# A decoder step on one core: the third normalization moved into the feed-forward before it, and the scan's opening rewritten

## What is computed

```
x = x + mixer(rmsnorm(x, norm_mix[layer]))
x = x + square(relu(rmsnorm(x, norm_mlp[layer]) @ w_up[layer])) @ w_down[layer]
```

```
z, xbc, dt = split(h @ w_in)            # h = rmsnorm(x), 1024 -> 2048 + 4096 + 32
xbc  = silu(causal_conv(xbc))           # four taps per channel, with history for the samples
dt   = softplus(dt + dt_bias)           # step sizes, one per head (32) and token
acs  = cumsum(dt * a) per chunk of 128  # exp(acs), exp(acs_end - acs), exp(acs_end): decays
# then, chunk after chunk, the scan over the states of 8 groups of 4 heads, gating by silu(z), norm
```

## Time and profile before

| | us |
|---|---|
| median of three runs | 3750.37 |
| profiled execution | 3743.06 |
| its span | 3741.4 |

### The profile page before, as it was taken

The page is one execution under the profiler, slowest core; times in us unless marked ns, Lnnn a source line. Parts: engine busy times, 40 slices in busy tenths (PEclk is TensorE's granted clock), DMA queues, the critical chain, the costliest instruction groups (busy, mean ns, idle before and its releaser), DMA issues. The chain is left out here.

```text
span 3741.4 us, 57050 instructions
## 1 busy us (share of the span) xinstructions
PE 3350.8 (90%) x20488; PEld 3116.8 (83%) x20488; DVE 1534.1 (41%) x2721; ACT 1138.1 (30%) x2092; POOL 1188.1 (32%) x849
## 2 busy tenths in 40 slices
PE   5779978975699999999679999999859999999998
PEld 5559963664599999999578888998849999999998
DVE  4489972333222121212336666666641221212122
ACT  3412212342332122222224555545531231312132
POOL 2015831212132222222215655545444322222222
PEclk9979988987799999999879999999969999999999
DMA  3017654003211111111232122222224111111111
GB/s 121 20 38 126 195 167 138 1 18 113 76 48 46 45 50 46 45 45 50 48 87 75 59 89 86 75 91 86 86 74 140 45 48 46 45 45 50 45 45 68
DMA packets 345874, 263.82 MB, mean 71 GB/s; under 512 B 55926, under 2 KB 311942, under 8 KB 344038
## 3 DMA queue, kind: packets, MB, share of 16 engines
q1 hardware_dynamic: 328102, 228.50, 20.7%
q10 hardware_dynamic: 10496, 15.81, 1.9%
q0 software_dynamic: 7168, 18.08, 1.4%
HBM read 219.43 MB, written 44.76 MB: 71 GB/s over the span
## 5 line engine op out<-in xcount | busy, mean ns | idle before, releaser
L232 POOL TENSOR_TENSOR w_low_sb<-w_loaded_sb,w_high_sb 128x1024 fp32r<-128x1024 f32 (+1 forms) x278 | 570.6, 2060 | 1761.2 <-ACT w_high_sb L224 1743.3
L250 PE MATMUL psum<-act_high_sb,w_high_sb 128*128 128x344 f32 (+1 forms) x2544 | 817.0, 321 | 24.0 <-PEq L188 17.1
L250 PE MATMUL psum<-act_low_sb,w_high_sb 128*128 128x344 f32 (+1 forms) x2544 | 815.3, 320 | 0.0
L250 PE MATMUL psum<-act_high_sb,w_low_sb 128*128 128x344 f32 (+1 forms) x2544 | 815.0, 320 | 0.0
L250 PE MATMUL psum<-second_high_sb,w_high_sb 128*128 128x344 f32 x1704 | 546.0, 320 | 0.0
L250 PE MATMUL psum<-second_low_sb,w_high_sb 128*128 128x344 f32 x1704 | 544.8, 320 | 0.0
L250 PE MATMUL psum<-second_high_sb,w_low_sb 128*128 128x344 f32 x1704 | 544.8, 320 | 0.0
L250 PEld LDWEIGHTS psum<-act_high_sb,w_high_sb 128*128 128x128 f32 (+1 forms) x2544 | 478.8, 188 | 26.0 <-issue 25.7
L250 PEld LDWEIGHTS psum<-act_high_sb,w_low_sb 128*128 128x128 f32 (+1 forms) x2544 | 479.2, 188 | 0.4
L250 PEld LDWEIGHTS psum<-act_low_sb,w_high_sb 128*128 128x128 f32 (+1 forms) x2544 | 478.7, 188 | 0.4
L224 ACT CAST w_high_sb<-w_loaded_sb 128x1024 fp32r<-128x1024 f32 (+1 forms) x230 | 239.9, 1043 | 671.3 <-PE psum L250 601.4
(11 more groups left out here) (419 smaller groups left out, 4655.3 us busy)
## 6 DMA issues: line engine op xcount, KB each, us to landing
w_loaded_sb<-in_w_up SPq DMA_DIRECT2D x64, 512.0 KB, 4.1
w_loaded_sb<-in_w_down SPq DMA_DIRECT2D x64, 512.0 KB, 3.7
w_loaded_sb<-in_w_in_odd SPq DMA_DIRECT2D x48, 512.0 KB, 4.0
key_pages_sb<-in_cache_k SPq DMA_DIRECT2D x64, 256.0 KB, 2.8
ecay_sum_spread_sb<-decay_sum_scratch SPq DMA_DIRECT2D x8, 2048.0 KB, 9.7
w_loaded_sb<-in_w_in_even SPq DMA_DIRECT2D x28, 512.0 KB, 4.1
x_scratch<-x_sb SPq DMA_DIRECT2D x2, 4128.0 KB, 13.2
x_sb<-x_scratch SPq DMA_DIRECT2D x2, 4128.0 KB, 14.9
```

Source lines behind the costliest of these rows:

```text
L232: ins = self.nc.gpsimd.tensor_tensor(self.wl[:, par, k, 0:width], self.wf[:, par, k, 0:width], self.wh[:, par, k, 0:width].bitcast(F32), A ...
L250: ins = nc.tensor.matmul(out, w[:, par, k, 0:width], a[:, k, cols], start=n == 0, stop=n == 3 * KT - 1)
```

## The change

1. **Normalization folded.** `layer_tail` of layer 0 gets `after=mixed`, a `Fold` for the third normalization, which writes its tiles into the pair of tiles `second`. The eight down units of the last group carry its work. `first_unit` gets a width, and the unit of the step sizes (32 columns) is it, inside `layer_tail`, with `act_rstd` behind.
2. **Small loads and the store moved.** `load_small` (ten of the small loads) stands on SP between the projection's loads and those of the feed-forward; `keep_x` stores x tile by tile behind the last down units, and loads the first two weights of the next block. The other three small loads (history, `expand`, the shifted samples) come in the next block, once unit 0 there is done.
3. **Opening.** Unit 0 of group 0 multiplies the unnormalized pair, and DVE multiplies by the root as it empties the banks. Beside it the normalized tiles are made, in place, and unit 1 takes them tile by tile (`second_unit`). ACT empties unit 1 after the softplus.
4. **Small work between the units.** History is turned before and after tile 6 (of 18 column tiles, i = 3 e + t), the step sizes after tile 9, sums and sample values after tile 11, the decays on ACT before the copy of tile 12. DVE does its shares between the convolutions.
5. `time_steps` and its block are gone; several buffers share other places.

```diff
...
+class Steps:
...
+    def load_small(self, sp):
...
+            for n, name in enumerate(("dt_bias", "a_log", "d_skip")):
+                sp.dma_start(self.sm[:, n:n + 1], B.i[name].rearrange("o h -> h o")).then_inc(self.s_small, 16)
+            for j in range(CW):
+                sp.dma_start(B.cw[:, :, j], B.i["conv_w"][0, j].rearrange("(c p) -> p c", p=P)).then_inc(self.s_small, 16)
...
+    def keep_x(self, sp):
+        B, u = self.B, self.u
+        for k in range(KT):
+            if k == KT - 2:
+                B.load_weights(sp, u, self.par, self.w_in[:, :, COL_DT:COL_DT + NH], NH)
+            if k == KT - 1:
+                B.load_weights(sp, u + 1, 1 - self.par, self.w_in[:, :, COL_X:COL_X + P])
+            sp.wait_ge(B.s_tile_free, (u - KT + k) * 3 + 9)
+            sp.dma_start(B.x_scratch[:, k, :], B.x[:, k, :]).then_inc(self.s_keep, 16)
...
+    def second_unit(self, pe):
...
+        for k in range(KT):
+            pe.wait_ge(self.s_high, k + 1)
+            self.await_low(pe, k)
             for t in range(NT):
...
+    def act_softplus(self, act):
...
+        nc.scalar.activation(self.raw[:], self.raw[:], ACT.Identity, bias=sm[:, 0:1]).then_inc(self.s_bias, 1)
...
+    def dve_normed(self, dve):
...
+        dve.wait_ge(self.s_keep, 16 * KT)
+        fold.await_rstd(dve)
+        for k in range(KT):
+            nc.vector.scalar_tensor_tensor(out=B.x[:, k, :], in0=B.x[:, k, :], scalar=B.gains[:, fold.gain, k:k + 1],
+                                           in1=fold.rstd[:], op0=ALU.mult, op1=ALU.mult).then_inc(self.s_normed, 1)
+            if k == 1:
+                for t in range(NT):
+                    B.await_tile(dve, self.u, t)
+                    nc.vector.tensor_tensor(self.raw[:, tcols(t)], B.tile(self.par, t, NH), fold.rstd[0:NH, tcols(t)],
+                                            ALU.mult).then_inc(self.s_raw, 1)
...
+            if k >= 1 and k - 1 not in self.POOL_K:
+                low(k - 1)
...
@@ mamba_groups, SP @@
+            def opening():
+                load_unit(0, 1)
+                load_unit(0, 2)
+                steps.load_history(sp)
+                for e in range(3, 6):
+                    load_unit(0, e)
+                steps.store_sums(sp)
+                load_unit(1, 0)
+                steps.await_stored(sp)
...
@@ mamba_groups, POOL @@
+            def opening():
+                steps.pool_low(pool, 0)
+                B.split_low(pool, unit(0, 1), par(1), pieces=2)
+                for k in steps.POOL_K[1:]:
+                    steps.pool_low(pool, k)
...
@@ mamba_groups, PE @@
+            def opening():
+                B.multiply(pe, unit(0, 0), par(0), steps.fold.high, steps.fold.low)
+                steps.second_unit(pe)
+                steps.turn_history(pe, 0)
+                for i in range(6, 18):
+                    tile(0, i // 3, i % 3)
+                    if i == 6:
+                        steps.turn_history(pe, 1)
+                    if i == 9:
+                        steps.turn_steps(pe)
+                    if i == 11:
+                        steps.sum_steps(pe)
+                pe.wait_ge(steps.s_sumc, 5)
+                pe.wait_ge(steps.s_chc, 2)
+                turn_conv_rows(0)
...
@@ mamba_groups, ACT @@
+            def opening():
+                high = lambda e: B.split_high(act, unit(0, e), par(e))
+                for k in range(KT):
+                    steps.act_high(act, k)
+                    if k == 2:
+                        high(1)
+                high(2)
+                steps.act_softplus(act)
+                act.wait_ge(B.s_tile_free, unit(0, 0) * 3 + 9)
+                for i in range(3, 18):
...
+                    if i == 12:
+                        steps.act_decays(act)
+                    evacuate(0, i // 3, i % 3, bank=3 * par(1) if i < 6 else 0)
...
@@ mamba_groups, DVE @@
+            def opening():
+                steps.dve_normed(dve)
+                for t in range(NT):
+                    B.await_tile(dve, unit(0, 0), t)
+                    nc.vector.tensor_tensor(pre[:, 0, PAD + t * TT:PAD + (t + 1) * TT], B.tile(par(0), t),
+                                            steps.fold.rstd[:, tcols(t)], ALU.mult).then_inc(B.s_tile_free, 1)
...
+                steps.dve_steps(dve)
+                steps.dve_history(dve)
+                convolve(0, 0)
+                steps.dve_rows(dve)
+                convolve(0, 1)
+                steps.dve_sums(dve)
+                convolve(0, 2)
+                steps.dve_decay(dve)
+                convolve(0, 3)
...
```

More of the change, by code:

```diff
@@ L700, in act @@
                 high(last, 0, 9 + k)
+            elif behind is not None:
+                behind()
             if self.after:
@@ L2193, in _ @@
             projected.act(act)
-            feed.act(act, kept=(lambda k: rows.kept(act, k)) if rows else None)
+            feed.act(act, kept=(lambda k: rows.kept(act, k)) if rows else None, behind=(lambda: steps.high_first(act)) if steps else None)
+            if steps:
+                steps.high_second(act)
+                after.act_rstd(act, steps.u)
             if rows:
@@ L2455, in part @@
                 if nx is not None:
-                    for e in range(0 if g is None else 1, 6):
+                    for e in range(1, 6):
                         load_unit(nx, e)
@@ L2501, in finish @@
                                gst[:]).then_inc(s_gout, 16)
+            def opening():
[3 more added lines that the diff above has]
+                    steps.pool_low(pool, k)
+                for e in range(2, 6):
+                    B.split_low(pool, unit(0, e), par(e), pieces=2)
+                B.split_low(pool, unit(1, 0), par(0), pieces=2)
+                pool.wait_ge(steps.s_dend, 1)
+                pool.wait_ge(steps.s_exp, 4)
             def part(g, nx, more):
-                splits = [] if nx is None else [0, 1, 2, 3] if g is None else [1, 2, 3]
+                splits = [] if nx is None else [1, 2, 3]
                 if g is not None:
```

446 lines of the change are left out of this document (264 added, 182 removed).

## The result

The changed kernel took 3683.93, 3686.55, 3690.90 and 3702.31 us, a median of **3688.7**; the kernel before took 3748.48 to 3753.21 in four runs, median 3750.2. The ratio is 0.984, with a 95% interval of 0.982 to 0.987. The forecast was 3691.8, and faster by 58.6; it is faster by 61.5.

What follows compares the result with a forecast made beforehand. Bound by TensorE, busy 90% of the span; gains lie where it stands still between first feed-forward and group scan. Stretch 162.5 to 103.9 us saves 58.6 from the 3750.37 median: 3691.8 us, range 3682 to 3705.

Steps and rivals of the forecast that it cites:

- Step sizes' unit with sums, 14.7: Unit of 32 columns right after the last down matmul, sums of squares included: 14.7 us without a gap.
- First unit 11.3, to 27.0: Group scan's first unit, on unnormalized tiles after the block change: 11.3 us without waiting for the normalization, ending at 27.0.
- Chain 22.9 + 4.0 = 26.9: Normalized tiles made beside the first unit: 22.9 us as before, 4.0 for added weight split and multiplies; last low tile 42.6.
- The copy behind the softplus frees the third unit, 47.7: ACT empties the second unit only after its softplus; the first copy frees a bank for the third unit at 47.7 us.
- Four units, small matmuls, clock: 45.2 + 8.5 + 2.5 = 56.2: Rest of the opening on PE: four units 45.2 us, small matmuls between them 8.5, clock loss after idling 2.5; end 103.9.
- Nothing from the convolutions, the decays, the small loads or the store: Other work in the opening, the early small loads and the tile-by-tile store of x stay covered: cost 0.
- C: Rival: early small loads make the feed-forward's first weights 14 us late, once; 3706 us; chance 0.03.
- 58.6 for the stretch: Last down matmul to conv-row transposes falls from 162.5 to 103.9 us, 58.6 less, all leaving the total.
- Rival A: Normalization's chain and ACT's queue take longer, as POOL's work can hold DVE: 7.2 us plus clock's 2.5; 3701; chance 0.15.
- B: Rival: small work between PE, DVE and ACT stalls the opening's units, 12.6 us more; 3704; chance 0.10.
- D: Rival: last eight down units lose weight lookahead, about 10 us each, 82 in all; slower, 3774; chance 0.02.
- E: Rival: copies not held by the softplus, small work at its best; opening ends at 97, no clock loss; 3685; chance 0.10.

Runs made afterwards that it cites:

- The run without a fall of the clock: Changed kernel with copies before softplus, all low halves on VectorE, second unit's weight split behind two normalized tiles: stretch 95.9 us, median 3691.5 us.
- the run with both edits: Changed kernel with ScalarE's copies of the second unit ahead of the softplus and all eight low halves on VectorE: stretch 100.9 us, median 3681.9 us.
- the run with the copy first: Changed kernel with ScalarE emptying the second unit's three tiles before the softplus: stretch 101.3 us, median 3696.5 us.

## Why the prediction was right

Its steps, from T = 0:

- **Step sizes' unit with sums, 14.7.** Measured 14.66, no wait. **Block change 1.0:** 0.64 on PE.
- **First unit 11.3, to 27.0.** It ended at 26.9.
- **Chain 22.9 + 4.0 = 26.9.** Measured 25.2. The added part was 2.3, not 4.0. The three multiplies took 2.0 of it (1833.87 to 1835.83), which leaves some 0.3 for GpSimd's weight split, given 2.4; no run takes that split out. The last low half came at 40.45 (42.6), ScalarE's last high one at 38.2 (40.4). The unit ended 4.3 us behind what PE alone would have taken, 3.2 of them waits in the trace, and not 5.7.
- **The copy behind the softplus frees the third unit, 47.7.** It was the copy, at 45.4; the 2.3 us are those of the chain and the block change.
- **Four units, small matmuls, clock: 45.2 + 8.5 + 2.5 = 56.2.** Measured 56.15, but the parts differ. The run without a fall of the clock took 95.93 - 41.30 = 54.6, so the clock cost 1.5. The small matmuls took 8.7 in the trace (from 1867.16, 1879.79 and 1888.57, each to the next unit's matmul) and the four units the other 45.9. One term was 1.0 too large, two together 0.9 too small: that this sum fits to 0.1 us is luck.
- **Nothing from the convolutions, the decays, the small loads or the store.** The last convolution ended 11 us ahead of VectorE's copy of the conv rows, no wait stands between the units, and C was refuted in this kernel and bounded by doubling the loads.
- **58.6 for the stretch.** It was 60.9, and the rest of the program gave 1.7 back, which no step had: the profiled execution was to take 3684.5 us and took 3683.9. The median lay 4.8 above it and not 7.3, which is the rest of the 3.1 us between 3691.8 and 3688.7. So the total came closer than its parts: the stretch was taken 2.3 us too long, and the rest of the program, taken as unchanged, cost 1.7 more.

Rival A needed GpSimd to hold the chain for longer, and it held it for less. B found no wait, D no gap in the last down units. E was near in time only (3685 is 3.7 us from the median, the forecast 3.1): the softplus did hold the copies. D's parts add up to 10.1 us a unit and 81 in all, not 82, which changes nothing.

What the parts are worth, undone one at a time: fold 21.3, unnormalized unit 9.3, small work between units 6.0, first weights ahead 4.1, and small loads early 16.5, measured on the kernel before. Together 57.2 of 60.9. The rest was not tried alone, and since the first weights show that parts hide behind one another, the near match of the sum is no proof that nothing else counts.

## What to carry to other kernels

Rebuild the stretch between two matmuls that both kernels have, term by term from one trace, and find what ends last at each point on each queue: that gave the gain of the stretch to 4% (58.6 for 60.9), before any luck in the whole time. VectorE operations with two operands in SBUF took 3.4 us for 1.25 beside GpSimd's here, and giving GpSimd half of the subtractions made the chain longer (25.2 us against 23.0); in such a case try the chain on VectorE alone. And where a wait on a bank's release lies behind a long piece of ScalarE work or behind a weight split, change the order in that queue before changing the work.

## What I had not expected of the hardware

- **The clock doesn't always fall at the same place.** The waits of the second unit (0.3, 0.3, 0.6 and 1.8 us) left the granted clock at 1.00 through all of that unit in one profile, and the fall came in the third unit, 0.9 us behind the wait of 1.75; the same program had it in the second unit's last step in another, 0.6 us behind the wait of 1.80. I forecast 2.5 us for the clock; a fall costs 1.5 here. In the one profile of the version with the shortest stretch, with 1.9 us of waiting in all, none came. After edits that shorten a wait, count the falls before judging the edit.
- **A stage that no edit touches moved the total by 22 us.** The last down matmul ended between 1811.9 and 1834.1 us in the runs of the changed kernel's relatives that have the same program up to there. The window from 900 to 1050 us, in the run with both edits and the run with the copy first:

```profile
900.00:1050.00 150.00, 115.10 (x686) 99.44 (x687) 39.65 (x49) 42.07 (x42) 29.83 (x14) 0.83 0.20 65
...
900.00:1050.00 150.00, 115.14 (x573) 93.33 (x573) 35.18 (x42) 37.02 (x37) 20.70 (x11) 0.68 0.17 58
```

  0.83 of the clock against 0.68 for identical code. Hence the profiled executions' times don't follow their stretches, and medians probably not either; why the clock differs there stays open.
- **The table load** of the softplus took 1.28 us, at 1858.76 in the changed kernel, and the next activation started 0.02 us behind it.
